# The last tap of the second token group's convolution, on GpSimd in place of VectorE

## The reference

```python
def short_conv(x, buf, w):
    L = x.shape[1]
    xp = jnp.concatenate([buf.astype(x.dtype), x], axis=1)
    y = sum(w[j] * xp[:, j:j + L] for j in range(CONV_W))
    return jax.nn.silu(y), xp[:, L:]
```

## Time and profile before

| | us |
|---|---|
| median of 3 runs | 2650.51 (2650.06 to 2651.29) |
| span of the profiled execution, first to last instruction | 2647.3 |
| PE busy | 2584.7 (98%) |
| DVE busy | 1380.3 (52%) |
| ACT busy | 1128.1 (43%) |
| POOL busy | 244.2 (9%) |

### The profile page before, as it was taken

One profiled execution on the slowest core, in us unless ns is written; L12 is line 12 of the kernel. 1 busy time (PEld: TensorE's weight loads), 2 busy tenths in 40 slices (PEclk: granted clock), 3 DMA queues, 4 the chain that ended last, 5 costly groups with the idle time before them and its releaser, 6 DMA issues.

```text
span 2647.3 us, 39319 instructions
## 1 busy us (share of the span) xinstructions
PE 2584.7 (98%) x16324; PEld 2307.5 (87%) x16324; DVE 1380.3 (52%) x2201; ACT 1128.1 (43%) x1914; POOL 244.2 (9%) x396
## 2 busy tenths in 40 slices
PE   8998999999999999999999999999999999999998
PEld 7778888788887798899999989998877888999998
DVE  4746765656564565434444465535544456454344
ACT  6654446455444245333333345433332345333324
POOL 4121111100001001100000001110000000000000
PEclk9999999999999999999999999999999999999999
DMA  6553335533333455533333245554444343333322
GB/s 205 157 156 106 104 113 135 154 101 85 106 95 92 120 144 168 170 120 112 105 95 111 83 131 151 165 150 123 120 120 146 102 121 122 87 111 106 96 88 82
DMA packets 368722, 321.47 MB, mean 121 GB/s; under 512 B 11930, under 2 KB 339668, under 8 KB 368545
## 3 DMA queue, kind: packets, MB, share of 16 engines
q1 hardware_dynamic: 336224, 207.91, 27.2%
q0 software_dynamic: 32320, 111.05, 13.8%
HBM read 261.33 MB, written 57.58 MB: 120 GB/s over the span
## 4 chain that ended last, share of the span: by engine, by line
PE 85%; DVE 6%; ACT 5%; DMA 2%; issue 2%; SPq 0%; POOL 0%; DVEq 0%; ACTq 0%; POOLq 0%
PE dense L605 75%; PE mixer L605 8%; ACT arena L1148 2%; DVE wlo L1665 1%; ACT whi L1148 1%; DMA wst<-in_w_in_even_dram 1%; DVE arena L1890 0%; DVE hf L1806 0%; ACT relu L1148 0%; ACT L1148 0%; DVE hlo L1802 0%; ACT L1153 0%; DMA arena<-xrow 0%; DVE arena L1892 0%; PE mixer L995 0%
## 5 line engine op out<-in xcount | busy, mean ns | idle before, releaser
L605 PE MATMUL dense<-hhi,whi 128*128 128x272 f32 (+1 forms) x3072 | 847.9, 330 | 22.0 <-DVE wlo L1665 15.3
L605 PE MATMUL dense<-hhi,wlo 128*128 128x272 f32 (+1 forms) x3072 | 824.9, 323 | 0.0
L605 PE MATMUL dense<-hlo,whi 128*128 128x272 f32 (+1 forms) x3072 | 824.2, 323 | 0.0
L1665 DVE TENSOR_TENSOR wlo<-wst,whi 128x1024 fp32r<-128x1024 f32 x384 | 471.7, 1228 | 233.2 <-ACT whi L1148 232.3
L605 PEld LDWEIGHTS dense<-hhi,whi 128*128 128x128 f32 x3072 | 515.8, 189 | 78.8 <-DVE wlo L1665 21.1
L1148 ACT ACTIVATE whi<-wst 128x1024 fp32r<-128x1024 f32 x384 | 403.8, 1052 | 423.9 <-PE dense L605 410.5
L605 PEld LDWEIGHTS dense<-hhi,wlo 128*128 128x128 f32 x3072 | 514.1, 189 | 41.7
L605 PEld LDWEIGHTS dense<-hlo,whi 128*128 128x128 f32 x3072 | 516.4, 189 | 37.4 <-issue 0.7
L605 PE MATMUL dense<-h1hi,whi 128*128 128x272 f32 (+1 forms) x1536 | 422.5, 329 | 9.3 <-DVE wlo L1665 5.0
L605 PE MATMUL dense<-h1hi,wlo 128*128 128x272 f32 (+1 forms) x1536 | 414.0, 324 | 0.0
L605 PE MATMUL dense<-h1lo,whi 128*128 128x272 f32 (+1 forms) x1536 | 412.1, 322 | 0.0
(11 more groups left out here) (352 smaller groups left out, 1813.6 us busy)
## 6 DMA issues: line engine op xcount, KB each, us to landing
wst<-in_w_ff_dram SPq DMA_DIRECT2D x256, 512.0 KB, 4.0
wst<-in_w_in_even_dram SPq DMA_DIRECT2D x48, 512.0 KB, 4.1
wst<-in_w_in_odd_dram SPq DMA_DIRECT2D x48, 512.0 KB, 4.0
proj<-ffh POOLq DMA_DIRECT2D x48, 272.0 KB, 2.6
proj<-ffh POOLq DMA_DIRECT2D x48, 256.0 KB, 2.3
arena<-proj POOLq DMA_DIRECT2D x16, 512.0 KB, 4.9
wst<-in_w_out_even_dram SPq DMA_DIRECT2D x16, 512.0 KB, 4.1
arena<-proj POOLq DMA_DIRECT2D x8, 1024.0 KB, 8.2
```

Source lines behind the costliest of these rows:

```text
L605: return pe.matmul(out, lhsT, rhs, start=start, stop=stop)
L1665: TT(wlo[:, u % 2, :], wst[:, u % 2, :], whi[:, u % 2, :].bitcast(F32), ALU.subtract)\
```

## The change

In group 1, DVE adds taps 0 and 1 only. At piece 3 it copies the tail columns out, which raises `conv_done`; POOL, before it sends the row, waits for this and does tap 2 in `last_tap`: it multiplies the columns of `xc2` by the weight in place (512 columns, then the 32 of the samples), waits for that, and adds them to `pout2` (512 columns, then 32). A new semaphore, `conv_taps`, counts these; DVE waits for it before it writes the older columns of the channel two further on. Where one semaphore more was needed, `ms_km` is folded into `gs_km`, which counts on. Group 0 and all of layer 1 stay as they were.

```diff
--- before.py
+++ after.py
@@ -1035,7 +1035,7 @@
                     mm(MB[0:n, 0, 0:DV + 1], m["ST"][0:n, h, :], V1[0:n, h, :], start=False, stop=True)\
                         .then_inc(S("ms_num"), 1)
                 elif step == "dc":
-                    pe.wait_ge(S("ms_km"), 2 * h + half + 1)
+                    pe.wait_ge(S("gs_km"), 2 * H + 2 * h + half + 1)
                     for b in range(4):
                         r = h * NB + 4 * half + b
                         if r >= 3:
@@ -1692,6 +1692,8 @@
                 if p == 0:
                     if g:
                         dve.wait_ge(S("conv_done"), ci - 1)
+                        if c >= 2:
+                            dve.wait_ge(S("conv_taps"), c - 1)
                         dve.tensor_copy(row[:, 0:3], before3[:, c, :])
                         if c == 0:
                             evac_wait(dve, ("misc", "csT"))
@@ -1701,20 +1703,21 @@
                 if j == 0:
                     evac_wait(dve, (u, 0))
                 w = par[:, 64 + j * NCONV + c:65 + j * NCONV + c]
+                if g and j == CONVW - 2:
+                    dve.tensor_copy(tails[:, c, 0:3], row[:, 512:515])
+                    dve.tensor_copy(tails[:, c, 3:27].rearrange("p (b s) -> p b s", s=3), smp[:, :, LS:LS + 3])\
+                        .then_inc(S("conv_done"), 1)
+                    return
                 ins = STT(y[:, 0:512], row[:, j:j + 512], w, y[:, 0:512], ALU.mult, ALU.add)
                 if g:
                     ys = y[:, 512:544].rearrange("p (b s) -> p b s", b=NB)
                     ins = STT(ys, smp[:, :, j:j + LS], w, ys, ALU.mult, ALU.add)
-                if j < CONVW - 2:
+                if j < CONVW - 2 - g:
                     link(ins)
                     return
                 ins.then_inc(S("conv_y"), 1)
                 if g == 0:
                     dve.tensor_copy(before3[:, c, :], row[:, 512:515]).then_inc(S("conv_done"), 1)
-                else:
-                    dve.tensor_copy(tails[:, c, 0:3], row[:, 512:515])
-                    dve.tensor_copy(tails[:, c, 3:27].rearrange("p (b s) -> p b s", s=3), smp[:, :, LS:LS + 3])\
-                        .then_inc(S("conv_done"), 1)
 
             def unit_begin(u):
                 kind, l, g, a, k = PLAN.units[u]
@@ -2194,7 +2197,7 @@
                 n = NS
                 def keys(h, q):
                     TT(m["KM"][0:n, q], bcm(m["KW"][0:n, h], [n, 4, P]),
-                       bcl(rowmask[:, 4 * q:4 * q + 4], [n, 4, P]), ALU.mult).then_inc(S("ms_km"), 1)
+                       bcl(rowmask[:, 4 * q:4 * q + 4], [n, 4, P]), ALU.mult).then_inc(S("gs_km"), 1)
 
                 if step == "km":
                     dve.wait_ge(S("g_kw"), TILES + 1)
@@ -2426,6 +2429,20 @@
                 n = GN[g]
                 dma(proj[l][c, :, G0[g]:G0[g] + n], pout2[:, i % 2, 0:n]).then_inc(S(f"stored{i % 2}"), 16)
 
+            def last_tap(u, c):
+
+                row, y = xc2[:, (NCONV + c) % 2], pout2[:, PLAN.in_rank[u] % 2]
+                j = CONVW - 2
+                w = par[:, 64 + j * NCONV + c:65 + j * NCONV + c]
+                pool.wait_ge(S("conv_done"), NCONV + c + 1)
+                x = row[:, j:j + 512]
+                smp = row[:, 515:XR].rearrange("p (b s) -> p b s", b=NB)[:, :, j:j + LS]
+                ys = y[:, 512:544].rearrange("p (b s) -> p b s", b=NB)
+                pool.tensor_scalar(x, x, w, None, ALU.mult)
+                step(pool.tensor_scalar(smp, smp, w, None, ALU.mult))
+                pool.tensor_tensor(y[:, 0:512], y[:, 0:512], x, ALU.add)
+                pool.tensor_tensor(ys, ys, smp, ALU.add).then_inc(S("conv_taps"), 1)
+
             def unit_end(key):
                 u = key[0]
                 kind, l, g, a, k = PLAN.units[u]
@@ -2434,6 +2451,9 @@
                 if u in PLAN.after_conv:
                     _, _, g_, c, _ = PLAN.units[u - 1]
                     pool.wait_ge(S("conv_y" if g_ else "conv_act"), g_ * NCONV + c + 1)
+                    if g_:
+                        last_tap(u - 1, c)
+                        pool.wait_ge(S("conv_taps"), c + 1)
                     send(u - 1, 0, g_, c)
                 if l or a >= NCONV:
                     evac_wait(pool, key)
```

## The result

| | before | after |
|---|---|---|
| median of 5 runs | 2650.51 us (2650.06 to 2653.57) | 2661.89 us (2660.69 to 2665.30) |
| span of the profiled execution | 2647.3 us | 2660.1 us |
| ratio of the medians, 95% interval | | 1.0044 [1.0031, 1.0056] |

What follows compares the result with a forecast made beforehand. PE was taken to bound everything behind 390 us, its idleness from 205 to 390 us ending on DVE. The channel terms summed to +4.45 us: a span of 2651.8, 2655.0 us with 3.2 added; range 2649.0 to 2660.5.

Steps and rivals of the forecast that it cites:

- What bounds it: PE bounds everything behind 390 us; from 205 to 390 us some 18 us of PE idleness end on DVE.
- The channels priced at nothing or near it: Channels 1, 2, 6 and 11 cost nothing, channel 7 +0.1 us, channel 10 -0.3 us.
- What is removed: Each tap taken off DVE gains 0.83 us, counting only where PE waits for DVE: channels 0, 3, 8 and 10.
- A tap is 2.5 us: POOL's time per channel: 0.65 + 0.20 + 0.1 + 1.30 + 0.25 us; 3.15 with the upper bound for the multiplication.
- The bound from affine selects: POOL's one-input instructions, 0.192 us for 8 columns and 0.289 for 128, put the 512-column multiplication at 0.60 us or more.
- I count every overlap as DVE's loss: Where DVE's two-SBUF-input instructions meet POOL's arithmetic, DVE waits and POOL keeps its length.
- Channels 4 and 5: L2546 runs under the inversion and channel 5's tap delays the spreading L1972: +2.0 us, bounds 0.3 and 2.9.
- The price of 0.3 to 1.0 us for the later send of channel 4: Channel 4's send, 2.8 us later, delays the emptying at 287.85 and PE: 0.3 to 1.0 us, inside the +2.0.
- Channels 0 and 3: Channel 0's tap holds DVE's masks and delays A of tile 1, +1.3 us; channel 3 adds +0.3 on A of tile 2.
- Channels 9 to 11: Channel 9, L1972 behind a tap, +0.15 us; channel 10, PE's wait before L1988 goes, -0.3; channel 11 nothing.
- rival 2: Relief of DVE wins: about -0.8 us, 2649.7, up to 5.3 gained if the clock stays; chance 0.25 together with rival 3.
- rival 1: Dearer taps, queues feeding each other: 7.7 us plus 2.5 for one uncovered channel, 2658 to 2661 us; chance 0.20 beyond +7.

Runs made afterwards that it cites:

- Relief: Changed kernel with the last tap of group 1 done by nobody: 2646.78 us, -3.8 us against the kernel before.
- Queue8: Only channel 8's tap moved off DVE, with POOL writing zeros three times in place of its arithmetic: 2648.37 us, -1.8 us against the kernel before.
- queue8long: Only channel 8's tap moved off DVE, with POOL writing zeros six times in place of its arithmetic: 2653.40 us, +2.9 us against the kernel before.
- queue: Changed kernel with POOL's four arithmetic instructions per tap replaced by three writes of zeros: 2652.57 us, +2.0 us against the kernel before.
- first4: POOL does the last tap of channels 0 to 3 only, the others as before: 2652.97 us, +2.1 us against the kernel before.
- Last4: POOL does the last tap of channels 8 to 11 only, the others as before: 2655.36 us, +4.5 us against the kernel before.
- ch8: POOL does the last tap of channel 8 only, the others as before: 2654.90 us, +4.0 us against the kernel before.

## Why the prediction was wrong

**What bounds it: right.** The second stretch is unchanged, and PE's long waits still end on `wlo` and the spreading.

**The channels priced at nothing or near it: right.** Channels 1, 2, 6, 7, 10 and 11 cost -1.1 us with an interval of the ratio that holds 1; forecast was -0.2 (channel 7's +0.1 and channel 10's -0.3).

**What is removed: about right.** Relief shows what this is worth alone, 3.8 us. The forecast had credited 0.83 each at channels 0, 3 and 8, and 0.3 at 10: 2.8.

**A tap is 2.5 us: wrong.** The term "multiplication 0.65, at most 1.30" measured 1.57 undisturbed (1.625 mean), "the 32 columns 0.20" 0.36, the wait of 0.1 before the addition is small, but one of 0.30 stands before each send, which the sum had left out. Undisturbed that is 3.5 us and 0.30. The bound from affine selects, at 0.8 ns a column, did not carry over: 480 columns more cost 1.21 us here, 2.5 ns each.

**"I count every overlap as DVE's loss": the step that failed.** It rested on one row, where `wlo` lost to L2546. Up to L912 the loss is shared about equally, 7.2 us on DVE and 6.6 on POOL. At channel 8 the inversion and `wlo` keep their length, DVE loses 0.7 us on the copy between them, and POOL loses 3.0 us (6.5 against 3.5). I had +1.2 us for DVE's delay there, and nothing for POOL's queue, since a tap from 345.3 to 347.8 would have been over before the copy at 349.84. A tap of 6.5 us is not. Queue8 shows that the reasoning stood with 3 us (-1.8), queue8long that it falls with 6.4 (+2.9).

**Channels 4 and 5: +2.0 became +4.5.** The chain is the one described, in dearer pieces. POOL and DVE of after:

```profile
283.68 1.57 POOL L2441 TENSOR_SCALAR ffh<-ffh,par 128x512 f32<-128x512 f32 x1
...
289.17 1.30 POOL L2566 TENSOR_TENSOR arena<-arena 128x512 f32<-128x512 f32 x1
...
289.22 2.14 DVE L1893 TENSOR_TENSOR arena<-arena 32x512 f32<-32x512 f32 x1
...
290.39 1.85 POOL L2508 DMA_DIRECT2D arena<-proj  x2
...
294.72 0.55 POOL L2552 DMA_DIRECT2D xrow<-arena  x1 [1.74 <-DVE arena L1970]
300.07 0.92 POOL L2554 DMA_DIRECT2D arena<-xrow  x1 [4.80 <-DMA xrow<-arena]
...
303.10 2.40 DVE L1975 TENSOR_TENSOR arena<-arena,blkmask 128x512 f32<-128x512 f32 x2 [3.80 <-DMA arena<-xrow]
```

The multiplication L2566 holds the inversion (2.14 us, and 1.07 at 353.54) as foreseen, and channel 5's addition the spreading (2.40 against 1.29). Not foreseen: the way out at 294.72 landed after 5.35 us, its wait 4.80 against 2.88. Ahead of it in POOL's queue are loads of the next tile, issued at 290.39, 4.3 us before it, since channel 4's tap stood in front of them; before it was 7.2 us (285.33 and 292.56). No run moves those loads alone, so this cause is argued, but every kept trace fits it. In the eight kernels with the loads issued 7.2 us ahead of the way out, the way back is issued 2.6 to 3.4 us after it; in the seven with 4.3 us, 4.9 to 5.5 us after it. One of the seven is queue, whose taps only write zeros, so this part is time in POOL's queue. The price of 0.3 to 1.0 us for the later send of channel 4 held: PE's wait for the emptying went from 0.29 to 1.24 us (at 291.48).

**Channels 0 and 3: +1.6 became +2.1** (first4, with an interval that holds 1), by the marks about 1 us each: channel 3's addition held the masks, L1924 took 2.17 us at 271.65 for 1.13, and I had +0.3 for it. Channel 0 was held from the other side than I wrote. POOL's tap took 4.2 us (212.11 to 216.27), and the two sends behind it put `arow` at 217.75, though A was ready at 215.05. In the time of before these are 218.8 and 216.1; I had A at 217.8 and POOL free at 217.0.

**Channels 9 to 11: small, as said.** Last4 costs 0.5 us more than ch8, within scatter. But channel 9's addition did hold the spreading, as channel 5's did (L1975 at 365.56 took 2.42 us for 1.29), where I had 0.45 us less a slack.

**The clock: a term left out.** Of the 12.5 us, 4.0 are PE being busier with the same matmuls; I had written that PE's busy time stays at what it was. The forecast looked at the clock only for gains (rival 2) and put no price on losing it: the waits of 3.83 us (0.84 before) and 4.25 us (none before) are each followed by eight matmuls in 2.07 us or more for which the earlier trace rows has 1.16. The granted clock (third number from the end) in the 4 us behind both, in windows of after, and behind the first of them in before:

```profile
304.90:308.80 3.90, 3.90 (x20) 3.90 (x21) 2.81 (x5) 1.06 (x1) 0.67 (x2) 0.59 0.18 71
367.40:371.50 4.10, 4.10 (x18) 4.10 (x19) 4.07 (x8) 0.00 (x0) 0.66 (x2) 0.50 0.43 132
```

```profile
299.80:303.70 3.90, 3.89 (x32) 3.89 (x33) 3.64 (x7) 1.06 (x1) 0.00 (x0) 1.00 0.01 1
```

0.50 is the lower of the two levels, 1.2 GHz, and 1.00 is 2.4 GHz.

**The rivals.** It went by rival 1, whose words (dearer multiplication, queues that feed each other) fit and whose price of 7.7 us plus one uncovered channel did not: no channel lost its cover, and the ones that were counted cost more than double (12.3 us for the six, where the sum had 4.65). That the total came within 1.2 us of rival 1's upper end is luck. The Trainium skill's rule ("SBUF — State Buffer", "Who interferes with whom"), that whichever issues first keeps the port for its whole instruction, would have had POOL wait at channel 8 behind the inversion; there the trace agrees (L1893 from 351.47, POOL's multiplication from 351.74, held 0.66 us). The +0.65 us that I worked out by it took only DVE's side of that and was further off than my own +1.2. And by the starts shown the rule is not the whole: the addition of 32 columns started 0.13 us before `wlo` and stood 1.85 us.

## What to carry to other kernels

Before a step goes to GpSimd, list what stands behind it in GpSimd's own queue, DMA issues first, and the slack of each: here 3 us fitted before the trip of tile 3 and 6.4 us cost 4.7 more. Price the step at its stretched length when VectorE works beside it from SBUF (6.5 us for 3.5), and charge contention to both sides, since one row shows only who lost that time. When a step is put off to let a trip pass, look at what waits for the step itself: here its send held a bank, and nothing was won. And a longer wait of TensorE can cost more than itself: a third of this loss was the same matmuls at a lower clock.

## What the runs showed of the hardware

- GpSimd's multiplication by a per-partition column took 1.57 us for 512 columns and 0.36 for 32, longer than the addition of two tensors (1.27 and 0.25).
- VectorE's short instructions are held as well, whole: one of 32x8 elements took 1.15 us beside an addition on GpSimd, where its like take 0.15 or 0.16. The rows are DVE's and POOL's of after:

```profile
285.69 0.16 DVE L1959 TENSOR_TENSOR arena<-arena 32x8 f32<-32x8 f32 x1
285.88 1.15 DVE L1960 TENSOR_TENSOR arena<-arena 32x8 f32<-32x8 f32 x1
...
285.71 1.30 POOL L2443 TENSOR_TENSOR ffh<-ffh 128x512 f32<-128x512 f32 x1
```

- A copy with one input was held too: L1970 took 1.09 us at channel 8, beside POOL's addition from 354.94, and 0.37 before, when POOL did nothing. The Trainium skill names copies among the instructions that can take the shared port ("SBUF — State Buffer", "Who interferes with whom"); the trace agrees.
